# Second block's first mixer in a new order: memory units among the weight slabs, convolutions one per two slabs, output projection from the memory's tiles on

## What is computed

```python
def mlstm_mixer(h, mem_n, w_in, conv_w, gate_bias, h_gain, w_out, w_mem_kv, mq_gain, mk_gain):
    p = h @ w_in
    qk = jax.nn.silu(causal_conv(p[..., :2 * W], conv_w))        # 12 tiles of 128 columns
    v = p[..., 2 * W:3 * W]                                      # 6 tiles
    o = p[..., 3 * W:4 * W]                                      # 6 tiles
    gates = p[..., 4 * W:4 * W + 2 * MLSTM_HEADS] + gate_bias
    q_mem = p[..., 4 * W + 2 * MLSTM_HEADS:]                     # 2 tiles
    cell = mlstm_chunkwise(heads(qk[..., :W]), heads(qk[..., W:]), heads(v), i_gate, f_gate)
    cell = rms_norm(cell, h_gain).reshape(B, S, W)
    h_a = jax.nn.sigmoid(o) * cell
    h_m = memory_cross_attention(q_mem, mem_n, w_mem_kv, mq_gain, mk_gain)
    return jnp.concatenate([h_a, h_m], axis=-1) @ w_out          # 8 tiles in, 8 out
```

## Time and profile before

| | |
|---|---|
| median of 3 runs | 2401.18 us (2399.24 to 2402.59) |
| the profiled execution's own time | 2406.21 us |
| its span, first to last instruction | 2404.8 us |
| PE busy over the span | 2340.7 us, 97% |
| DVE, ACT busy | 1629.1 us (68%), 1236.4 us (51%) |
| mean granted clock of TensorE | 0.990 |
| this mixer, from the end of its head to the start of f5 | 1494.83 to 1670.13 us |

### The profile page before, as it was taken

One profiled execution on the slowest core, in us unless ns is written; L12 is line 12 of the kernel. 1 busy time (PEld: TensorE's weight loads), 2 busy tenths in 40 slices (PEclk: granted clock), 3 DMA queues, 4 the chain that ended last, 5 costly groups with the idle time before them and its releaser, 6 DMA issues.

```text
span 2404.8 us, 45379 instructions
## 1 busy us (share of the span) xinstructions
PE 2340.7 (97%) x18642; PEld 2288.2 (95%) x18642; DVE 1629.1 (68%) x2889; ACT 1236.4 (51%) x2052; POOL 61.9 (3%) x114
## 2 busy tenths in 40 slices
PE   8999999999999999999999999888999999989999
PEld 7999999999999999999999999887999999978999
DVE  6655987776486578778657865755765767574764
ACT  5444565554454455656445654645544645455642
POOL 2001100000000011000000000000000010000000
PEclk9999999999999999999999999998999999999999
DMA  7654634565566554347656655433765676533753
GB/s 207 177 175 128 174 98 122 138 187 169 167 169 176 177 150 125 105 131 207 188 185 166 180 189 162 133 97 82 208 183 176 177 200 197 155 100 83 207 185 132
DMA packets 583438, 382.77 MB, mean 159 GB/s; under 512 B 19977, under 2 KB 559091, under 8 KB 583232
## 3 DMA queue, kind: packets, MB, share of 16 engines
q1 hardware_dynamic: 580080, 376.78, 54.2%
q0 software_dynamic: 3152, 3.08, 0.5%
HBM read 378.67 MB, written 1.07 MB: 158 GB/s over the span
## 4 chain that ended last, share of the span: by engine, by line
PE 86%; DVE 8%; ACT 3%; issue 2%; DMA 1%; SPq 0%; DVEq 0%; ACTq 0%
PE bank L605 85%; DVE wlo L2023 2%; ACT whi L1340 1%; DVE ry L2042 1%; DVE ry L2040 1%; PE bank L936 0%; DVE ybuf L2073 0%; DMA wraw<-in_w_ffn_gu 0%; DVE smh L2459 0%; DVE ssum L2035 0%; DVE xlo L2056 0%; DVE hT L2077 0%; PE bank L704 0%; DVE a_qk L2570 0%; DVE rst L2044 0%
## 5 line engine op out<-in xcount | busy, mean ns | idle before, releaser
L2023 DVE TENSOR_TENSOR wlo<-wraw,whi 128x1024 fp32r<-128x1024 f32 (+1 forms) x713 | 862.7, 1217 | 274.9 <-ACT whi L1340 271.6
L1340 ACT ACTIVATE whi<-wraw 128x1024 fp32r<-128x1024 f32 (+1 forms) x713 | 744.2, 1052 | 582.5 <-DMA wraw<-in_w_ffn_gu 168.0
L605 PE MATMUL bank<-xhi,whi 128*128 128x256 f32 (+2 forms) x3880 | 577.5, 289 | 11.3 <-DVE xb L2486 3.9
L605 PE MATMUL bank<-xhi,wlo 128*128 128x256 f32 (+2 forms) x3880 | 563.2, 285 | 6.4 <-DVE wlo L2023 6.4
L605 PE MATMUL bank<-xlo,whi 128*128 128x256 f32 (+2 forms) x3880 | 554.1, 284 | 0.0
L605 PEld LDWEIGHTS bank<-xhi,whi 128*128 128x128 f32 (+1 forms) x3880 | 511.9, 190 | 22.1 <-ACT xhi L1378 6.1
L605 PEld LDWEIGHTS bank<-xhi,wlo 128*128 128x128 f32 (+1 forms) x3880 | 509.2, 189 | 9.5 <-DVE wlo L2023 9.0
L605 PEld LDWEIGHTS bank<-xlo,whi 128*128 128x128 f32 (+1 forms) x3880 | 504.6, 188 | 0.2
L605 PE MATMUL bank<-act_hi,wlo 128*128 128x256 f32 (+1 forms) x1408 | 400.5, 284 | 0.0
L605 PE MATMUL bank<-act_lo,whi 128*128 128x256 f32 (+1 forms) x1408 | 400.5, 284 | 0.0
L605 PE MATMUL bank<-act_hi,whi 128*128 128x256 f32 (+1 forms) x1408 | 398.6, 283 | 0.0
(11 more groups left out here) (419 smaller groups left out, 1840.9 us busy)
## 6 DMA issues: line engine op xcount, KB each, us to landing
wraw<-in_w_ffn_gu SPq DMA_DIRECT2D x176, 512.0 KB, 3.9
...
```

Of the source, the lines that this page charges most:

```text
L605: return E.matmul(out_, lhsT, rhs, start=first, stop=last, skip_group_check=True)
L1340: A.activation(flat(whi, u), flat(wraw, u), ACT.Copy).then_inc(S("hi"), 1)
L2023: V.tensor_tensor(flat(wlo, u), flat(wraw, u), flat(whi, u).bitcast(F32), ALU.subtract).then_inc(lo_ready[u % RING], 1)
```

## The change

Nothing is computed otherwise; the same instructions are put in another order, and some results go to other places in PSUM.

- The head now takes the gates, the memory's q and two v tiles (`A_HEAD`). The q and k slabs are spread evenly among the other 27 (`A_ORDER`), so that the twelve convolutions come one per slab or one per two slabs, one step behind their slab, where three or four came at once at the start. The gates' work comes at step 5 instead of 2.
- The four cells start at steps 10, 15, 20, 25 instead of 6, 11, 16, 21.
- The eight memory units run from step 13 on, among the slabs, instead of from step 24 on. Their scores go to the upper half of bank 2, whose lower half takes the gate row of the cells, and their transposes to the upper half of bank 6, whose lower half takes the turned v tiles. For that each score waits until DVE has read the gate row of every cell begun so far (`a_w` >= 2 x `c.mub`), and each gate row waits for the exps of the scores before it (`mem_e`).
- The output projection of the first four `awo` slabs takes the memory's tiles first (k = 6, 7, then 0 to 5: `A_CELL_ROWS`), in banks 0, 1, 6 and 7. `gated`, `high` and `low` of the first three cell tiles are done while the last two `ao` slabs are multiplied; the last cell's mean square comes between k = 6 and k = 7.

The core of the diff:

```diff
@@ -133,21 +133,23 @@
-A_HEAD = [("ag", 0), ("aqk", 0), ("aqk", 1), ("aqk", 6)]
-A_ORDER = ([("aqk", 7), ("av", 0), ("aqk", 2), ("av", 1), ("aqk", 8), ("mkv", 2), ("aqk", 3), ("av", 2), ("aqk", 9), ("mkv", 0), ("aqk", 4), ("aq", 0),
-            ("aqk", 10), ("av", 3), ("aqk", 5), ("av", 4), ("aqk", 11), ("mkv", 3), ("mkv", 1), ("aq", 1), ("av", 5)] + [("ao", i) for i in range(6)])
+A_HEAD = [("ag", 0), ("aq", 0), ("av", 0), ("av", 1)]
+A_ORDER = ([("aqk", 0), ("aqk", 6), ("mkv", 0), ("aqk", 1), ("mkv", 2), ("aqk", 7), ("aq", 1), ("aqk", 2), ("mkv", 1), ("aqk", 8), ("mkv", 3), ("aqk", 3),
+            ("aqk", 9), ("av", 2), ("aqk", 4), ("aqk", 10), ("av", 3), ("av", 4), ("aqk", 5), ("aqk", 11), ("av", 5)] + [("ao", i) for i in range(6)])
...
-A_VALUES = [key for key in A_ORDER if key[0] == "av" or key[0] == "mkv" and key[1] >= 2]
-A_NORMS = [key for key in A_ORDER if key[0] == "aq" or key[0] == "mkv" and key[1] < 2]
-A_STEP = {key: 2 + i for i, key in enumerate(A_ORDER)}
-A_CONV_STEP = [2, 2, 3] + [A_STEP["aqk", i] + 1 for i in A_CONV[3:]]
+A_VALUES = [key for key in A_HEAD + A_ORDER if key[0] == "av" or key[0] == "mkv" and key[1] >= 2]
+A_NORMS = [key for key in A_HEAD + A_ORDER if key[0] == "aq" or key[0] == "mkv" and key[1] < 2]
+A_STEP = {key: max(1, 2 + i - len(A_HEAD)) for i, key in enumerate(A_HEAD + A_ORDER)}
+A_CONV_STEP = [A_STEP["aqk", i] + 1 for i in A_CONV]
...
-A_CELL_STEP = (6, 11, 16, 21)
-A_MEM_STEP = 24
+A_CELL_STEP = (10, 15, 20, 25)
+A_MEM_STEP = 13
+A_GATE_STEP = 5
+A_CELL_ROWS = (6, 7, 0, 1, 2, 3, 4, 5)
...
-A_BANK = (0, 1, 2, 3, 5, 4, 6, 7)
+A_BANK = (0, 1, 6, 7, 2, 3, 4, 5)
...
@@ -990,20 +992,25 @@
+                E.wait_ge(S("mem_o"), 2)
...
-                for k in range(6):
-                    E.wait_ge(S("a_cellh"), k + 1)
+                for n, k in enumerate(A_CELL_ROWS):
+                    if k < 6:
+                        E.wait_ge(S("a_cellh"), k + 1)
...
-                        if k == 0:
+                        if n == 0:
...
-                        mm(bank[A_BANK[d]][:, 0:T], slab(whi, u)[:, k, :], cellp[0][:, k, :], k == 0, False)
+                        mm(bank[A_BANK[d]][:, 0:T], slab(whi, u)[:, k, :], cellp[0][:, k, :], n == 0, False)
...
-                        if k == 0:
+                        if n == 0:
...
-                    E.wait_ge(S("a_cellp"), k + 1)
+                    if k < 6:
+                        E.wait_ge(S("a_cellp"), k + 1)
...
-                        mm(bank[A_BANK[d]][:, 0:T], slab(whi, u)[:, k, :], cellp[1][:, k, :], False, False)
+                        m = mm(bank[A_BANK[d]][:, 0:T], slab(whi, u)[:, k, :], cellp[1][:, k, :], False, n == KD - 1)
+                        if n == KD - 1:
+                            m.then_inc(S("used"), 1)
...
@@ -1041,7 +1050,10 @@
+                    if c.scored > 0:
+                        E.wait_ge(S("mem_e"), c.scored)
...
+                    c.mub += 1
...
@@ -1085,44 +1097,40 @@
-                        if i == 0:
-                            E.wait_ge(S("a_wk"), 2 * ML_HEADS)
-                        else:
+                        E.wait_ge(S("a_w"), 2 * c.mub)
+                        if i > 0:
...
-                        mm(bank[4][:, 0:T], a_qm[:, pair, t0:t0 + n], a_km[:, h, :], True, True).then_inc(S("mem_s"), 1)
+                        mm(bank[2][:, T:2 * T], a_qm[:, pair, t0:t0 + n], a_km[:, h, :], True, True).then_inc(S("mem_s"), 1)
...
-                        if g == 0:
-                            E.wait_ge(S("tv_c"), tv0 + 8)
-                        else:
+                        E.wait_ge(S("tv_c"), c.tv)
+                        if g > 0:
...
-                        if g == 0:
-                            E.wait_ge(S("hn_out"), hn0 + 4)
-                        elif tl == 0 and hh == 0:
-                            E.wait_ge(S("mem_o"), pair)
+                        if tl == 0 and hh == 0:
+                            E.wait_ge(S("tv_c"), tv0 + 1 + A_VALUES.index(("mkv", 2 + pair)))
+                            if pair == 0:
+                                E.wait_ge(S("hn_out"), hn0 + 4)
+                            else:
+                                E.wait_ge(S("mem_o"), pair)
...
-            E.wait_ge(S("mem_o"), 2)
...
-            for d in range(KD):
+            for d in range(A_EARLY, KD):
...
-                if d < A_EARLY:
-                    products(bank[A_BANK[d]][:, 0:T], u, slab_cols(u, 0, P), xo, n_k=2, first=False, k0=6).then_inc(S("used"), 1)
-                    continue
-                if A_BANK[d] == 4:
-                    E.wait_ge(S("mem_e"), MEM_N)
...
@@ -2526,20 +2544,33 @@
+                    if (name, i) == ("ao", 4):
+                        V.wait_ge(S("a_cn"), 3)
+                        V.wait_ge(S("evac"), c.first + A_TAKEN["ao", 2] + 1)
+                        for k in range(3):
+                            gated(k)
+                    if (name, i) == ("ao", 5):
+                        for k in range(3):
+                            low(k)
...
+                yield
+                V.wait_ge(S("evac"), c.proj)
+                gated(3)
+                low(3)
+                yield
...
-                V.wait_ge(S("evac"), c.proj)
-                gated(0)
-                for i in range(6):
-                    if i < 5:
-                        gated(i + 1)
-                    low(i)
-                    yield
-                lo_until(AT["awo", 0, 0] + RING)
+                for k in (4, 5):
+                    gated(k)
+                for k in (4, 5):
+                    low(k)
+                    yield
+                for d in range(A_EARLY, KD):
+                    lo_until(min(AT["awo", 0, d] + 1, AT["awo", 0, 0] + RING))
+                    yield
...
-                while c.step < 2:
+                while c.step < A_GATE_STEP:
```

48 lines of the change are left out of this document (30 added, 18 removed).

## The result

The changed kernel took 2389.08 us (median of 4 runs, 2386.33 to 2390.43), the kernel before on the same chip 2401.89 us (4 runs, 2399.24 to 2405.14): a ratio of 0.9945, with a 95% interval of 0.9927 to 0.9962. Forecast were 2379.0 us, 2370 to 2391. So it is faster, and the time is in the range, but little more than half of the 22 us that I promised is there, and 2389.08 lies above the 2374 to 2384 of my own case. A second comparison, on another chip, gives 2388.09 us (5 runs) against 2404.93 us (9 runs), ratio 0.9932 (0.9918 to 0.9945), 16.8 us.

What follows compares the result with a forecast made beforehand. PE, 97% busy, bounds the kernel; idle time and low clock lose 39.0 us from head's end to f5. With 17.1 us of losses left, 21.9 is gained: 2406.2 to 2384.3, less 5.0 for the median, 2379.3; range 2370 to 2391.

Steps and rivals of the forecast that it cites:

- The costs at nothing: DMAs in the stretch, same in number and order of freeing, mean share 0.42, were costed at nothing, covered by seven-slab ring.
- Start: Front of the stretch: PE at the norm's mean waits 2.6 us for DVE's results and ACT's square; bounds 0 to 3.9.
- Gates: Eighth slab: PE waits 3.7 us for the sixth slab's result behind DVE's heap, plus 2.0 for low clock.
- Second cell: Step 15: the unit's score waits 3.1 us for DVE's weights (`a_w`), plus 2.0 for low clock, bounds 0 to 2.4.
- Third cell: Same wait for DVE's weights, without a convolution in its chain and with one more transpose on PE: 1.5 us.
- Second cell's mean square: PE waits 1.3 us for DVE's maximum and ACT's square, which comes behind the silus of head 2.
- Low clock: Half-speed PE after long waits, expected behind 3.25 us but not 2.71: 2.0 us each at gates and second cell.
- Tail: Last `ao` slab to fifth output slab: about 14 us against 34.3, with 0.9 us of waits left and nothing more late.
- A rule weighed: Skill's 2.66 us per table switch would add 2.8 us at the second cell's mean square, giving 2382.1; the trace's 1.29 was used.
- rival 2: More small waits among the units' steps as three engines hand over: 8 to 12 us, 2387 to 2391; chance 0.19.
- Rival 1: Clock stays up and the front waits less: 27 to 31 us won, 2370 to 2374; chance 0.15.
- rival 4: Scores' waits for `a_w` bring low clock again and again in steps 13 to 20: 18 us slower, 2419; chance 0.05.

Runs made afterwards that it cites:

- second execution: The changed kernel run and profiled again, nothing edited: median 2388.09 us, profiled 2388.75, stretch from the head's end to f5 158.61 us.
- the weights-first version: Against the changed kernel, DVE makes a new cell's weights ahead of the last cell's Newton step and cell tile: 2384.22 us, ratio to the kernel before 0.9908.
- the version with the silus last: Against the changed kernel, ACT does a cell's silus last in their step, behind the copy of the memory's transposed tile: 2392.46 us, ratio to the kernel before 0.9945.

## Why the prediction was right, and where it was off

**What bounds the kernel.** Right, and it decided: 39.0 us were lost in the stretch, and the gain came from there. **The costs at nothing**: right for this profile; behind f5 both take 734.7 us (which is luck in part, since others take up to 740.3), and the DMA share rose to 0.47 without a slab being late among those waits. In the second execution one slab is late at the start, by 0.53 us, and the wait behind it is 0.42 longer.

**The sum.** 17.1 us were to be left of the losses. The stretch of 157.60 less 136.3 of work makes 21.3, 4.2 more: 15.07 idle, where my terms have 13.1, and 6.2 from the low clock, where I had 4.0. Term by term:

- *Start* 2.6: measured 2.21 (2.63 in the other execution). *Gates* 3.7: 2.77 (3.58), with the heap on DVE that I had listed. *Second cell* 3.1: 3.06, on DVE's order as I had it, which the weights-first version shows. *Third cell* 1.5: 1.65. The last result, 0.5: 0.52. These steps were right because each was two engines' rows counted to the same event.
- *Second cell's mean square* 1.3: the time is there, 2.04, the waiter is another. PE meets the value turn first, which needs the unit's tile copied out of the bank's other half (`mem_c`). I had counted what the silus delay for their own cell, not for what else ACT has in that step. The cell's last square, 0.35: nothing.
- *Missed*: 0.78 behind the second cell, ACT's copy of a value turn, late by DVE's `xb`; 0.46 at f5, which the window before has in its own way; and 1.37 at the fourth output slab. I wrote that nothing more is late in the tail, by looking at tiles and not at the last `wlo`, which the change itself puts behind three splits.
- *Low clock.* The step that failed: "2.71 didn't bring it, 3.25 did". I took two spells of 2.0 us; there were four, behind 2.21, 2.77, 3.06 and 1.37, which cost about 1.5 each. The one in the tail can be priced by comparison: from the first cell tile to f5, without the wait at f5 itself, the changed kernel's two executions take 27.85 us, and four other profiles with the same order and waits there but no spell 26.2, so it cost 1.6. No length divides them: the 1.37 us in the tail is followed by a spell in five profiles (the changed kernel's two among them) and not in four, the 2.04 us at `sqb` in three and not in eight, and the 3.06 us in eight and not in one. What decides it stays open.
- *Tail* "about 14 us" against 34.3: 16.84. The wait for the `wlo` and its spell, 1.37 + 1.6, are the difference. The credit I gave to the three tiles being ready was wrong; the memory's rows do that work.

**A rule weighed.** A load and the activation behind it are 1.29 us apart at 1577.23 as well, and 1.30 us in both switches of the version with the silus last (1575.72 to 1577.02, 1578.91 to 1580.21), where nothing else is waited for. It is 1.29 or 1.30 us behind every such load in all 14 profiles. "ScalarE: Activation LUTs" (section "What ACT_TABLE_LOAD costs") of the Trainium skill has 2.66 us for a switch. No row of these traces agrees with that. By it the copy at 1578.85 would have come some 1.4 us later than its row, and not 2.8, since the 1.53 us wait for the convolution would have covered the first switch.

**The profile against the median.** I took off 5.0 us because the profiled 2406.2 lay above the median of 2401.2. In 48 later runs of the kernel before (2399.9 to 2411.8) it is near the middle (28 are below it), and the changed kernel's profile is 1.2 us below its own median. Of the 10.1 us between 2379.0 and 2389.08, this is 5.0 + 1.2. The sum is 3.5 of it (4.2 too little left in the stretch, 0.9 gained ahead of it, which is chance, and 0.2 beside), rounding 0.3.

**The rivals.** The time is in rival 2's range (2387 to 2391), and in mine only because I had stretched it to take that in. Its reason holds for little: of the waits only 0.78 and 2.04 come from other work in a unit's step, at two of the eight units, and the larger waits are my case's. Rival 1 fell with the low clock; rival 4 asked for low clock in steps 13 to 20, and there is one spell. The front, up to the step on the gates, did win little, as that step says.

**Where the gain came from, as far as it is shown.** The memory's rows first are worth 3.5 us by the medians, 2.4 to 3.4 in the stretch. The early gating isn't worth anything: it costs the 1.37 and saves 0.37 + 0.77. What is left, about 14 us of the stretch's 17.7, belongs to the units' move and to the new order of slabs and convolutions together, and no run takes the two apart. The rows say what each removed: the tail lost the units' waits, and ahead of it the two waits behind heaps of convolutions and norms (4.49 and 3.25 us) went, which made room for the units' work. That the spread convolutions did this, and not the units, is read from those rows and not shown by an edit. The units' move wasn't undone by itself, since in the new order of banks they can't stand in the tail.
